# Stick-breaking attention with queries on the partitions: sums by VectorE scans instead of TensorE products, heads written out, column blocks spread over them

## What is computed

```python
z = einsum('bhqd,bhkd->bhqk', qb, kb) * scale
strict = k_pos[None, :] < q_pos[:, None]
log_beta = log_sigmoid(z)
log_one_minus = where(strict, log_sigmoid(-z), 0.0)
suffix = cumsum(log_one_minus, axis=3, reverse=True) - log_one_minus   # over the keys
weights = where(strict, exp(log_beta + suffix), 0.0)
out = einsum('bhqk,bhkd->bhqd', weights, vb)
```

## Time and profile before

| | |
|---|---|
| median of 3 runs | 805.91 us (803.88 to 807.9) |
| profiled execution | span 803.9 us from the first to the last instruction; its own time is the same number to 0.1 us, as far as the times shown tell, and is 2.0 us under the median |
| TensorE busy (PE) | 767.7 us, 95% |
| VectorE busy (DVE) | 445.2 us, 55% |
| ScalarE busy (ACT) | 297.1 us, 37% |
| GpSimd busy (POOL) | 318.3 us, 40% |
| DMA share over the span | 29.7% |
| chain that ended last | PE 74%, DVE 16%, issue 5%, ACT 3% |

### The profile page before, as it was taken

How to read it: one execution, slowest core, us unless ns; L and a number is a source line. 1 busy time by engine, 2 the same in 40 slices (tenths; PEclk the granted TensorE clock), 3 DMA queues, 4 the chain that set the end, 5 groups by cost and what they waited for, 6 DMA issues and landing times.

```text
span 803.9 us, 9927 instructions
## 1 busy us (share of the span) xinstructions
PE 767.7 (95%) x3544; PEld 638.9 (79%) x3544; DVE 445.2 (55%) x534; ACT 297.1 (37%) x406; POOL 318.3 (40%) x135
## 2 busy tenths in 40 slices
PE   7999899899899989999699999999999999999996
PEld 6888788778788768777488988888888888888885
DVE  5437769887976996799566211222211123444467
ACT  5223455444455446564011433233333334323410
POOL 5444333341343322299100444444444444444710
PEclk9999899999899999999799999999999999999998
DMA  7223242323224311355200222322322224522102
GB/s 286 103 105 110 77 124 84 104 78 104 79 77 130 104 53 30 144 220 183 78 1 1 105 82 100 104 89 94 104 97 86 104 104 135 233 104 82 49 27 79
DMA packets 26391, 81.52 MB, mean 101 GB/s; under 512 B 3328, under 2 KB 3584, under 8 KB 26368
## 3 DMA queue, kind: packets, MB, share of 16 engines
q1 hardware_dynamic: 26368, 81.22, 29.7%
HBM read 71.77 MB, written 2.10 MB: 92 GB/s over the span
## 4 chain that ended last, share of the span: by engine, by line
PE 74%; DVE 16%; issue 5%; ACT 3%; DVEq 0%; DMA 0%; ACTq 0%; SPq 0%
PE ps L987 73%; DVE mT_lo L669 2%; DVE mT_hi L878 2%; DVE sb_lo L669 1%; DVE fx_nmax L770 1%; DVE qk_lo L669 1%; DVE mg_t L875 1%; DVE sb_t L783 1%; DVE fx_p L818 1%; ACT fx_p L537 1%; DVE mg_t L870 1%; PE ps L1139 1%; ACT sb_t L520 1%; ACT sb_t L518 1%; ACT sb_t L516 1%
## 5 line engine op out<-in xcount | busy, mean ns | idle before, releaser
L396 POOL TENSOR_TENSOR w_lo<-w_raw,w_hi 128x1024 fp32r<-128x1024 f32 x110 | 272.1, 2475 | 389.1 <-ACT w_hi L456 383.3
L456 ACT ACTIVATE w_hi<-w_raw 128x1024 fp32r<-128x1024 f32 x109 | 115.6, 1061 | 240.2 <-DMA w_raw<-w_stream_in 235.4
L987 PE MATMUL ps<-x1T_hi,w_hi 128*128 128x512 f32 (+1 forms) x376 | 141.3, 376 | 0.0
L987 PE MATMUL ps<-x1T_lo,w_hi 128*128 128x512 f32 (+1 forms) x376 | 141.2, 375 | 0.0
L987 PE MATMUL ps<-x1T_hi,w_lo 128*128 128x512 f32 (+1 forms) x376 | 141.2, 375 | 0.0
L950 DVE SCALAR_TENSOR_TENSOR conv<-ps,col,conv 128x511 f32<-128x511 f32 (+1 forms) x44 | 32.9, 748 | 166.7 <-ACT conv L632 163.7
L987 PE MATMUL ps<-xT_hi,w_hi 128*128 128x512 f32 x264 | 107.9, 409 | 2.6 <-DVEq L852 2.6
L987 PE MATMUL ps<-xT_lo,w_hi 128*128 128x512 f32 x264 | 104.9, 397 | 0.0
L987 PE MATMUL ps<-xT_hi,w_lo 128*128 128x512 f32 x264 | 104.8, 397 | 0.0
L987 PEld LDWEIGHTS ps<-x1T_lo,w_hi 128*128 128x128 f32 x376 | 70.8, 188 | 12.9
L987 PEld LDWEIGHTS ps<-x1T_hi,w_lo 128*128 128x128 f32 x376 | 70.8, 188 | 12.8
(11 more groups left out here) (154 smaller groups left out, 1209.2 us busy)
## 6 DMA issues: line engine op xcount, KB each, us to landing
w_raw<-w_stream_in SPq DMA_DIRECT2D x109, 512.0 KB, 3.2
wout_raw<-w_out_in SPq DMA_DIRECT2D x8, 512.0 KB, 4.8
q_stack<-qk_hi SPq DMA_DIRECT2D x28, 128.0 KB, 2.3
r_raw<-w_stream_in SPq DMA_DIRECT2D x5, 512.0 KB, 8.8
xT_raw<-xT_in SPq DMA_DIRECT2D x8, 256.0 KB, 6.8
x<-x_tok_in SPq DMA_DIRECT2D x4, 512.0 KB, 3.8
ln_rows<-rows_in SPq DMA_DIRECT2D x4, 512.0 KB, 5.7
out_dram<-x SPq DMA_DIRECT2D x8, 256.0 KB, 2.0
```

The source lines that it names most:

```text
L396: nc.gpsimd.tensor_tensor(w_lo[:, slot, :], w_raw[:, slot, :], plain(w_hi[:, slot, :]), ALU.subtract).then_inc(lo_ready, 1)
L456: nc.scalar.activation(w_hi[:, slot, :], w_raw[:, slot, :], ACT.Copy).then_inc(hi_ready, 1)
L987: return nc.tensor.matmul(out_, lhs, rhs, start=start, stop=stop, skip_group_check=True)
```

## The change

The stick-breaking scores are computed with queries on the partitions, in the same layout as the forgetting scores. The sum over the keys then runs along a row: VectorE makes it with four scans per head that run backwards over the keys (of 128, 256, 384 and 512 columns), each with two inputs in SBUF, `sb_t` (ln(1 + exp(-|z|))) and the new `sb_r` (relu(z)). ScalarE makes `sb_r` by one more pass. VectorE subtracts the sums from the scores in PSUM, ScalarE takes the Exp, TensorE transposes the weights (ten transposes, as for the other branch), ScalarE makes their high part out of PSUM and VectorE their low part.

The triangle and square of minus ones, the tiles `later`, and all their splits go. All eight heads are written out instead of a loop. Heads 0 to 7 have 3, 4, 3, 4, 3, 4, 4, 3 column blocks, and the shares of the four fills in rows are 5, 9, 5, 5 for three blocks and 5, 12, 8, 7 for four. The last pair uses the stacked copies like the others. `sb_o_low` and `sb_o_sum` lie in a place of their own; `sb_hi` shares its place with `sb_t` and `sb_lo` with `sb_r`.

```diff
-SB_OFF = [0, 640, 1024, 512]
-FX_OFF = [896, 1024, 512, 0]
+KEY_OFF = [0, 640, 1024, 512]
+QUERY_OFF = [896, 1024, 512, 0]
+SHARES = {4: (5, 12, 8, 7), 3: (5, 9, 5, 5)}
...
@@ SyncE
+            for h in range(HALVES):
+                for k in range(len(FILLS[h])):
+                    load_when_free(FIRST[h] + 3 + k)
                     if k == 0:
                         sp.wait_ge(sb_scored, h + 1)
                         sp.wait_ge(qk_split, pair * 4 + 4)
                         stack(e, 1)
+                if h < HALVES - 1:
+                    sp.wait_ge(fx_scored, h + 1)
+                    sp.wait_ge(qk_split, (h + 1) // 2 * 4 + 2)
+                    stack(1 - e, 0)
...
@@ ScalarE
+            def fill(h, k):
+                if k < len(FILLS[h]):
+                    high_in_order(FIRST[h] + k + 3)
+                    read_fill(h, k)
...
-                act.wait_ge(o_split[0], h + FREE)
+                if h > 0:
+                    act.wait_ge(sb_w_split, h)
+                    act.wait_ge(sb_mixed, h)
                 act.wait_ge(sb_scored, h + 1)
-                nc.scalar.activation(sb_t[:], ps[:, SB_PS:SB_PS + FLAT], ACT.Abs).then_inc(sb_absed, 1)
+                nc.scalar.activation(sb_t[:], scores, ACT.Abs).then_inc(sb_absed, 1)
+                nc.scalar.activation(sb_r[:], scores, ACT.Relu).then_inc(sb_relued, 1)
...
+                fill(h, 0)
+                act.wait_ge(sb_logged, h + 1)
+                nc.scalar.activation(sb_t[:], sb_t[:], ACT.Exp).then_inc(sb_weighed, 1)
...
+                fill(h, 1)
+                act.wait_ge(sb_turned, h + 1)
+                nc.scalar.activation(sb_hi[:], scores, ACT.Copy).then_inc(sb_w_hi, 1)
+                fill(h, 2)
                 act.wait_ge(fx_turned, h + 1)
                 nc.scalar.activation(fx_hi[:], ps[:, FX_PS:FX_PS + FLAT], ACT.Copy).then_inc(fx_w_hi, 1)
+                fill(h, 3)
...
@@ VectorE
+                dve.wait_ge(sb_relued, h + 1)
+                dve.wait_ge(sb_lned, h + 1)
+                for r in range(SB):
+                    keys = slice(QUERY_OFF[r], QUERY_OFF[r] + P * (r + 1))
+                    nc.vector.tensor_tensor_scan(sb_t[:, keys][:, ::-1], sb_t[:, keys][:, ::-1], sb_r[:, keys][:, ::-1],
+                                                 0.0, ALU.add, ALU.add).then_inc(sb_summed, 1)
+                dve.wait_ge(sb_summed, (h + 1) * SB)
+                nc.vector.tensor_tensor(sb_t[:], ps[:, SB_PS:SB_PS + FLAT], sb_t[:],
+                                        ALU.subtract).then_inc(sb_logged, 1)
...
-                nc.vector.tensor_copy(sb_hi[:], sb_t[:]).then_inc(sb_w_hi, 1)
                 dve.wait_ge(sb_w_hi, h + 1)
-                split_lo(sb_lo[:], sb_t[:], sb_hi[:]).then_inc(sb_w_split, 1)
+                split_lo(sb_lo[:], ps[:, SB_PS:SB_PS + FLAT], sb_hi[:]).then_inc(sb_w_split, 1)
...
@@ TensorE
-                pe.wait_ge(sb_soft_split, h + 1)
-                for part in (sb_hi, sb_lo):
-                    for o in range(0, FLAT, 512):
-                        end = min(o + 512, FLAT)
-                        product(ps[:, SB_PS + o:SB_PS + end], neg_tri[:], part[:, o:end])
-                pe.wait_ge(later_split, h + 1)
-                for part, soft in ((later_hi, sb_hi), (later_lo, sb_lo)):
...
+                pe.wait_ge(sb_weighed, h + 1)
+                turned(SB_PS, sb_t).then_inc(sb_turned, 1)
                 fill(2)
...
+                pe.wait_ge(fx_normed, (h + 1) * SB)
+                turned(FX_PS, fx_p).then_inc(fx_turned, 1)
                 fill(3)
```

More of the change, by code:

```diff
@@ L45, with fills_of_halves @@
 N_PAIR = N_QK0 + 4
-N_LAST = N_PAIR + 8 * (PAIRS - 1)
-N_MERGE = N_LAST + 4
+def fills_of_halves():
+    fills, gate = [], 0
+    for h in range(HALVES):
+        if h % 2 == 1 and h < HALVES - 1:
+            fills.append([("qk", j) for j in range(4)])
+        else:
+            n = 4 if h == HALVES - 2 else 3
+            fills.append([("gate", gate + i) for i in range(n)])
+            gate += n
+    assert gate == NG
+    return fills
+FILLS = fills_of_halves()
+FIRST = [N_PAIR + sum(map(len, FILLS[:h])) for h in range(HALVES + 1)]
+SHARES = {4: (5, 12, 8, 7), 3: (5, 9, 5, 5)}
+N_MERGE = FIRST[HALVES]
 N_UP = N_MERGE + KB
@@ L317, in _ @@
                     stack(0, 0)
[L319 to L324, removed]
+            for h in range(HALVES):
+                pair, e = h // 2, h % 2
+                for k in range(len(FILLS[h])):
+                    load_when_free(FIRST[h] + 3 + k)
                     if k == 0:
@@ L410, in _ @@
             pool.wait_ge(v_ready, 2 * SB)
[L411 to L417, removed]
+            for h in range(HALVES):
+                if h % 2 == 0:
+                    v_low(h // 2)
+                for n in range(FIRST[h] + 3, FIRST[h + 1] + 3):
+                    if n <= N_MERGE:
+                        low(n, n % 4)
             with pool.Fori(0, 2) as i:
@@ L561, in _ @@
             act.wait_ge(v_ready, 2 * SB)
[L562 to L576, removed]
+            for h in range(HALVES):
+                half(h)
             table(SET_SIGMOID)
-            act.wait_ge(sb_mixed, HALVES + FREE)
-            act.wait_ge(fx_mixed, HALVES + FREE)
+            act.wait_ge(sb_mixed, HALVES)
+            act.wait_ge(fx_mixed, HALVES)
             for d in range(KB):
@@ L1052, in masked, with half @@
                 return last
-            def half(pair, e, blocks, turn, first):
-                h = pair * 2 + e
-                n0 = turn + first
-                b0 = turn + (first - N_QK0)
+            def half(h):
+                pair, e = h // 2, h % 2
                 hd = slice(HEAD_DIM * e, HEAD_DIM * (e + 1))
-                order = sorted(blocks)
-                shares = (KB,) * 4 if len(order) == 4 else LAST_SHARES
+                blocks, shares = FILLS[h], SHARES[len(FILLS[h])]
+                read_before = FIRST[h] - N_QK0
                 def fill(place):
@@ L1096, in half, with turned @@
[L1096 to L1097 removed]
+                def turned(base, weights):
+                    for r in range(SB):
+                        for c in range(r + 1):
+                            o = base + KEY_OFF[c] + P * (r - c)
+                            last = nc.tensor.transpose(
+                                ps[:, o:o + P], weights[:, QUERY_OFF[r] + P * c:QUERY_OFF[r] + P * (c + 1)], ident[:])
+                    return last
@@ new lines, in half @@
+                pe.wait_ge(qk_split, pair * 4 + 2)
+                if h == 0:
+                    pe.wait_ge(v_ready, 2 * SB)
+                    pe.wait_ge(f_mined, 1)
+                    pe.wait_ge(f_absed, 1)
+                else:
+                    pe.wait_ge(sb_w_split, h)
+                pe.wait_ge(stack_in, h * (2 * STACK) + STACK)
+                for q, k, first in ((q_stack[:], k_stack[:], True), (qk_lo[hd, 0, :], qk_hi[hd, 1, :], False)):
+                    for r in (3, 2, 1, 0):
+                        o, width = SB_PS + QUERY_OFF[r], P * (r + 1)
+                        product(ps[:, o:o + width], q[:, P * r:P * (r + 1)], k[:, 0:width], start=first and r > 0)
```

292 lines of the change are left out of this document (88 added, 204 removed).

## The result

| | before | after |
|---|---|---|
| median | 805.91 us | 812.51 us (810.62 to 817.75, 7 runs) |
| ratio to before | | 1.0103, 95% interval 1.0072 to 1.0133 |
| span of the profiled execution | 803.9 us | 816.0 us (its own time 817.75) |
| TensorE busy | 767.7 us | 762.3 us |
| VectorE busy | 445.2 us | 419.5 us |

The kernel is 1.0% slower, though TensorE and VectorE both have less to do. The ratio is worked out over all runs of both kernels and is not the quotient of the two medians, which is 1.0082. The after profile is one of the slower of the seven runs, so its 12.1 us over before's profile are more than the 6.6 us between the medians; I use it for places and durations, and ratios and medians for prices.

A forecast was written before the change was run, and what follows sets the result against it. TensorE was taken to bound the kernel, with the ScalarE, VectorE and GpSimd chain nearly as long. Heads summed to 255 us plus 10 for the clock: 265 against 253.6, +11, so 815 us, range 796 to 823.

The forecast's parts named there:

- the 265 of the sum: Stage from TensorE's first scores to the merge: 255 us by heads plus 10 for the clock, against 253.6 before.
- the 10 us for the clock: Matmuls at the lower clock behind seven waits of about 2.4 us ahead of the second mixes, 1.5 us each.
- TensorE's own work: TensorE in the stage: sums go, transposes come, fewer products in the last pair; 8.6 us gained if only this counted.
- The scans collide: VectorE's scans: one 2.4 us GpSimd operation comes between two scans, ending them at T+12.5 (T = head's first scores), not T+10.1.
- Three-block heads: Heads 2, 4, 7: TensorE waits 1.6 us for `sb_t`, 1.4 for `fx_p`, 2.4 for `fx_lo`; 30.65 us plus clock.
- Odd heads: Four-block odd heads: 32.8 us plus clock, 0.6 less than before, still waiting for `fx_lo` ahead of the second mix.
- Head 0: First head: wait for VectorE's queue goes, but waiting for the forgetting scores' copies becomes 4.3 us; 34 us with lower clock.
- the merge counter: Start-up increment moved behind the heads: no cost at the merge was forecast.
- the sign turns on where the scans end: Whole kernel: slower if the scans end at T+12.5, faster at T+10.1, no difference at about T+11.
- scans that don't wait: Rival: scans don't wait for GpSimd, everything is 2.3 us earlier, stage 248 us, kernel 798 us; chance 0.35.
- a fixed wait of 2.4 us in four heads: Three-block heads' end: ScalarE reads block 2 before the forgetting weights' high part, so TensorE waits 2.4 us for `fx_lo`.
- backward scans at twice the price: Rival: backward scans cost double, 3.1 us more ahead of everything, eight times; kernel 830 us; chance 0.07.

The follow-up runs named there:

- e3: The changed kernel with GpSimd held in each head until the four scans are done: 803.76 us, ratio 0.9982 to the kernel before.
- e4: The changed kernel without ScalarE's Relu pass, softplus made by VectorE from PSUM, scans with one SBUF input: 803.59 us, ratio 0.9984 to the kernel before.
- e5: The changed kernel; in three-block heads ScalarE makes the forgetting weights' high part before reading block 2: 800.53 us, ratio 0.9934 to the kernel before.
- e12: The changed kernel with sums on TensorE and the old block spread; written-out heads, stacked copies, late merge counter kept: 811.29 us, ratio 1.0093 to the kernel before.
- e6: The changed kernel with three rows moved ahead of the forgetting scores (shares 8, 6, 5, 5 and 8, 9, 8, 7): 813.32 us, ratio 1.0097 to the kernel before.
- e10: The changed kernel with old block spread, one-SBUF-input scans, early merge counter, and last two heads' shares 4, 7, 2, 3: 787.75 us, ratio 0.9783 to the kernel before.

## Why the prediction was right, and where not

The forecast was 815 us in 796 to 823 and slower; the medians say 812.5. The growth was forecast too large, 11 us against 6.6 between the medians, and the range was wide enough to hold both signs. The stage took 263.2 us against the 265 of the sum. By heads (us; the forecast is without the 10 us for the clock, but head 0 has 3.0 of clock in it):

| head | 0 | 1 | 2 | 3 | 4 | 5 | 6 | 7 |
|---|---|---|---|---|---|---|---|---|
| blocks | 3 | 4 | 3 | 4 | 3 | 4 | 4 | 3 |
| forecast | 34 | 32.8 | 30.65 | 32.8 | 30.65 | 32.8 | 30.7 | 30.65 |
| measured | 36.3 | 32.8 | 31.7 | 33.0 | 31.6 | 33.0 | 30.9 | 33.8 |

That the stage came so near was in part luck. With TensorE's own work at full clock as in the forecast (216.8 us), its sum held 35.2 us of waits and 13 of lower clock; the profile has 32.4 and, as the rest, 14.0. Of the 32.4, 5.1 us are waits that I had not seen (`issue`, the merge counter, 0.3 for `qk_t`), so those that I had named are 27.3 and were put 7.9 too high. These misses nearly cancel. Point by point:

- **TensorE's own work is not what counts.** Right. Its busy time fell by 5.4 us and the stage grew.
- **The scans collide.** Right in place and size: the sum had one 2.4 us operation between two scans, the four ending at T+12.5; in head 1 they end at 126.49, which is T+12.4 (0.3 us later at the start, and 5.1 us long instead of 5.5). The weights were to be ready at T+15.3; they were at 129.33, T+15.3. Price: e3 and e4.
- **Three-block heads.** The sum had 1.6 us for `sb_t`, 1.4 for `fx_p`, 2.4 for `fx_lo`. Measured in head 2: 0.3, 1.5 and 2.2, and none of the 0.8 for the copies that the sum had in every head; the odd heads and head 6 have that. The first is smaller because a wait that I had not seen (1.4 us for the output's sum, heads 2 and 4) had already delayed the fills. Heads 2 and 4 took 31.7 and 31.6 us against 30.65 and clock. Head 7 took 33.8, with the merge counter's wait of 1.9 us at its end.
- **Odd heads.** 32.8 us and clock; they took 32.8, 33.0, 33.0. The place was right: in head 1 the second mix starts at 145.53, T+31.5, as in the sum. The wait ahead of it is 1.3 us, not 2.4, since TensorE came there later, at the lower clock left by head 0's wait. So the clock's 1.5 us per head did not come on top; they took the wait's place.
- **Head 0.** 34 us; it took 36.3. The wait for the copies was put at 4.3 us and measured 5.1 (the scores start 1.4 us earlier, the copies don't). More of the miss is clock, 3.0 us in the sum and 4.4 by the rest: the forgetting scores and two rows behind that wait run at the lower level (granted clock 0.50 from 88.64 to 92.90), and so does the second mix behind the wait for `fx_lo` (0.50 from 111.64 to 114.05).
- **Missed altogether:** the merge counter, a term put at nothing. The diff shows `sem_inc(merged, FREE_MERGE)` moved behind the heads; I counted that as nothing, and TensorE waited 1.9 us there. Missed too: in three-block heads the bank of the first fill is now the one whose output is added up last.
- **Clock, 10 us.** With the 3.0 of head 0 it is 13 us, and the rest of the profiled stage is 14.0, so the size is about right for that run. But the same rest is 12.8 us in the stage before: the clock hardly grew. Of the stage's 9.6 us, TensorE's own work gives -8.6, the waits +17.0 and the clock +1.2. e3 and e4, with nearly the same waits (23.2 and 23.1 us), leave rests of 9.1 and 12.4, so a rest is known to some 3 us only, and 12.8 against 14.0 is no difference.
- **Which case decides the sign.** Here the prediction was wrong though the number was not. It said that the sign turns on where the scans end, and gave 798 us to scans that don't wait. Measured without the collision: 803.8 and 803.6, which is 0.2% under the kernel before, at the edge of the intervals. Its stage of 248 us was near (249.1 in e3, 252.3 in e4), but from other parts: heads 2 and 4 were to take 28.6 us and took 30.0 to 30.5, each still with its 2.2 us for `fx_lo`, and the time behind the stage stayed over 472 us with the merge counter's wait ahead of it. e5, which takes away the 2.2 us and leaves the collision, has these two heads at 28.2. And with the collision the scans are still worth 1.1 to 1.9% against the sums on TensorE. The loss comes from what was put beside them: ScalarE's order in the three-block heads (1.7%, e5), which was in the sum as a fixed wait of 2.4 us in four heads and never stood among the rivals, and 0.9% of small things (e12).

One rival's sum does not add up: backward scans at twice the price were given 830 us, but 8 x 3.1 us on top of 815 are 840 before anything hides. The scans in e3, 1.20 us for 512 columns, rule that rival out.

The 0.9% of e12 was not taken apart by runs. Its profile puts it into the last two heads, the copies' waits and the merge counter; what each of these costs in time stays open.

## What to carry to other kernels

When a filler block is moved or dropped, walk every engine's queue for the first thing behind the place where it is read: a read that waits for the end of the fill must not stand ahead of a pass that the next product needs. Price a wait only where nothing later in the same stage is bound to another chain (e6 and e10 moved 6 us of waits and gained none). A counter's start-up increment that moves is an edit too: ask who waits for it. Before a VectorE operation gets two SBUF inputs, look at what GpSimd does at that time, and whether one operand can stay in PSUM.

## What had not been expected of the hardware

- A scan whose second operand is only passed over (bypass) costs the same, 1.194 us for 512 columns, as one that adds two operands, 1.198. Scans that run backwards cost what the forward one did (1.22 us); 128, 256, 384 and 512 columns take 0.43, 0.67, 0.93 and 1.20 us, so 0.26 us for each 128 columns and 0.16 beside.
- A collision stretches both sides, and in the rows it looks like taking turns: in the odd heads GpSimd's weight block starts together with the 384-column scan and takes 3.13 us where it took 2.41 alone, while that scan keeps its time; the 512-column scan behind it takes 2.2 us more. That they alternate is read from one pattern of starts and was not tested by a run.
